# Hybrid SSD, attention and MoE block: the last two units' rows added by one-hot matrices on PE, the other rows read during these units

## What is computed

```python
    _, eidx = lax.top_k(jnp.where(emask, biased, -jnp.inf), TOP_K)        # TOP_K = 6
    w = w / jnp.sum(w, axis=-1, keepdims=True) * ROUTE_SCALE
    out = (jax.nn.silu(n @ s_gate) * (n @ s_up)) @ s_down                 # shared expert
    for e in range(N_EXPERTS):                                            # 64
        hid = jax.nn.silu(n @ e_gate[e]) * (n @ e_up[e])
        out = out + (hid @ e_down[e]) * combine[:, e:e + 1]
    ...
        h = h + g2 * ff.reshape(bsz, t, d)
    return rms_norm(h, final_g)
```

## Time and profile before

| | |
|---|---|
| median of 3 runs | 1293.59 us (1291.52 to 1294.53) |
| the profiled execution's own time | 1292.14 us |
| its span, first to last instruction | 1290.4 us |
| busy: PE, DVE, ACT, POOL | 92%, 37%, 19%, 15% |
| HBM read, written | 314.49 MB, 26.82 MB |

### The profile page before, as it was taken

How to read it: one execution, slowest core, us unless ns; L and a number is a source line. 1 busy time by engine, 2 the same in 40 slices (tenths; PEclk the granted TensorE clock), 3 DMA queues, 4 the chain that set the end, 5 groups by cost and what they waited for, 6 DMA issues and landing times. The chain is left out here.

```text
span 1290.4 us, 13395 instructions
## 1 busy us (share of the span) xinstructions
PE 1187.4 (92%) x4803; PEld 611.3 (47%) x4803; DVE 480.3 (37%) x994; ACT 246.4 (19%) x611; POOL 196.2 (15%) x320
## 2 busy tenths in 40 slices
PE   4999999998999999999999999999989999967866
PEld 2535864555554444458854444444434444423322
DVE  4686035655566211104764222233222322212225
ACT  2141122233441000001121111112111211111101
POOL 5000021111002000010351212221212121211100
PEclk9999999999999999999999999999999999988988
DMA  9742242213449232337256999999999999999647
GB/s 300 192 131 65 66 137 93 90 42 131 131 131 307 84 130 66 96 104 315 93 204 265 346 421 421 423 423 421 413 409 410 395 400 403 377 388 421 268 189 289
DMA packets 108105, 322.28 MB, mean 250 GB/s; under 512 B 14500, under 2 KB 67832, under 8 KB 81032
## 3 DMA queue, kind: packets, MB, share of 16 engines
q1 hardware_dynamic: 87824, 269.37, 54.6%
q0 software_dynamic: 18688, 47.30, 10.4%
q10 hardware_dynamic: 1528, 4.77, 1.0%
HBM read 314.49 MB, written 26.82 MB: 264 GB/s over the span
## 5 line engine op out<-in xcount | busy, mean ns | idle before, releaser
L1795 PE MATMUL ps<-gu_hi,xsT 128*64 128x512 f32 (+1 forms) x704 | 241.8, 614 | 30.1 <-DMA gu_hi<-in_exp_w_up_dram 11.6
L1795 PE MATMUL ps<-gu_lo,xsT 128*64 128x512 f32 (+1 forms) x320 | 145.8, 609 | 9.8 <-issue 6.0
L1795 PEld LDWEIGHTS ps<-gu_hi,xsT 128*64 128x64 f32 (+1 forms) x704 | 84.6, 155 | 140.2 <-issue 138.6
L1335 DVE SCALAR_TENSOR_TENSOR hid<-ps,wgt,gated 128x256 f32<-128x256 f32 x42 | 20.3, 484 | 306.9 <-ACT gated L913 306.9
L1803 PE MATMUL ps<-dn_hi,hidT 128*64 128x512 f32 (+1 forms) x352 | 119.9, 597 | 1.3 <-DVE hn L1331 1.1
L1442 PE MATMUL ps<-n1T,ring 128*128 128x512 f32 x256 | 111.9, 593 | 0.0
L1672 PE MATMUL ps<-n1T,ring 128*128 128x512 f32 x256 | 110.9, 592 | 0.7 <-ACT attT L857 0.7
L688 POOL DMA_INDIRECT expert_rows<-hn,meta x42 | 41.9, 998 | 412.8 <-DVE hn L1331 371.0
L1331 DVE TENSOR_TENSOR hn<-ps,g_row 128x1024 f32<-128x1024 f32 x42 | 51.4, 1225 | 95.2 <-PE ps L1803 95.2
L913 ACT ACTIVATE gated<-ps 128x256 f32<-128x256 f32 x42 | 16.1, 384 | 333.2 <-PE ps L1795 333.2
L1795 PEld LDWEIGHTS ps<-gu_lo,xsT 128*64 128x64 f32 (+1 forms) x320 | 51.1, 165 | 60.3 <-issue 59.8
(11 more groups left out here) (331 smaller groups left out, 1341.6 us busy)
## 6 DMA issues: line engine op xcount, KB each, us to landing
gu_hi<-in_exp_w_gate_dram SPq DMA_DIRECT2D x44, 1024.0 KB
gu_hi<-in_exp_w_up_dram SPq DMA_DIRECT2D x44, 1024.0 KB
dn_hi<-in_exp_w_down_dram SPq DMA_DIRECT2D x44, 1024.0 KB, 29.2
ring<-in_w_in_dram SPq DMA_DIRECT2D x21, 1024.0 KB, 5.5
gu_lo<-in_exp_w_gate_dram SPq DMA_DIRECT2D x20, 1024.0 KB
gu_lo<-in_exp_w_up_dram SPq DMA_DIRECT2D x20, 1024.0 KB
dn_lo<-in_exp_w_down_dram SPq DMA_DIRECT2D x20, 1024.0 KB
h<-in_ada_w_dram POOLq DMA_DIRECT2D x32, 512.0 KB, 4.8
```

Source lines behind the costliest of these rows:

```text
L1795: ins = pe.matmul(ps[rows, 2 + b, :], xsT[:, b, k, rows], gu(s)[:, :, k, :], start=(k == 0), stop=(k == KC - 1))
```

## The change

What it does, engine by engine:

- U4 and U5 are not scattered. In a round, POOL scatters the earlier round's U4 at step 0, and nothing at step 5; after the loop nothing is left to scatter.
- Since rows of these units are no longer written, ACT fills all of `expert_rows` with zeros after attention, with six 2 MB DMAs from the tile `state`, which POOL sets to zero. SP and POOL wait for them after the merge.
- SP waits for the scatters up to U3 only, then reads tiles 0 and 1 (slots 0 and 4), then final_g, then tiles 2 and 3 (slots 2 and 5). Each tile's reads wait for the units that used their slots.
- POOL writes a row of numbers 0 to 511. DVE compares it with the token number of each row of U4 and U5, which gives a 128x512 one-hot matrix for each, and adds rows 0 and 1 of tile 0 to `h`, all of it ahead of the copy of U5's rows.
- PE multiplies these matrices with `ys`, so U4's and U5's rows go to their tokens in PSUM, and adds rows 4 and 5 (tile 3: row 5) with the identity. DVE adds the other rows to `h` one by one.

```diff
--- before.py
+++ after.py
@@ -288,7 +288,10 @@
         sh_hidT = scratch[:, T * FF:T * FF + 4 * P].rearrange("p (b j c) -> p b j c", b=2, j=2)
         taken = scratch[:, 2 * FF:4 * FF].rearrange("p (t q) -> p t q", t=T)
         blank = hn[:, T - 1, :]
-        junk = gu(FIXED).rearrange("p a k f -> p (a k f)")
+        spread, junk = (gu(SLOT[SEQ0 + LAST + T + i]).rearrange("p a k f -> p (a k f)") for i in range(2))
+        spread = spread[:, 0:2 * SEQ].rearrange("p (b t) -> p b t", b=2)
+        numbers = marks[:, 0:SEQ]
+        ON_PE = ((4, 5), (4, 5), (4, 5), (5,))
         fin_g = xsT[:, 0, :, :].rearrange("p k c -> p (k c)")
 
         widths = [KC * NE, NE, TOPK * NE, NE, RGROUPS * 8, RGROUPS * RGROUPS, RGROUPS * RGROUPS, P, RGROUPS * RGROUPS,
@@ -365,6 +368,7 @@
         gu_ready, gate_done, hid_done = sem("gu_ready"), sem("gate_done"), sem("hid_done")
         ht_ready, hT_done, ey_ready, ey_dve = sem("ht_ready"), sem("hidT_done"), sem("ey_ready"), sem("ey_dve")
         tail_sum, fsq_in, fin_done, stored = sem("tail_sum"), sem("fsq_in"), sem("fin_done"), sem("stored")
+        zeroed, numbered, spread_done = sem("zeroed"), sem("numbered"), sem("spread_done")
         block = ctx.enter_context(nc.Block())
 
         def block_used(n):
@@ -385,7 +389,8 @@
 
         def two_rows(t, part):
 
-            return flat(dn(t)) if part == 2 else gu(t)[:, part, :, :].rearrange("p k f -> p (k f)")
+            s = SLOT[SEQ0 + LAST + t]
+            return flat(dn(s)) if part == 2 else gu(s)[:, part, :, :].rearrange("p k f -> p (k f)")
 
         def rows_in_part(t, part):
 
@@ -448,6 +453,7 @@
                 load_block(n)
 
             sp.wait_ge(merged_done, KC)
+            sp.wait_ge(zeroed, 16 * TOPK)
             sp.dma_start(r_w[:, :, :], a["router_w"][0].rearrange("(p k) e -> p k e", k=KC)).then_inc(small_in, 16)
             sp.dma_start(r_b, a["router_bias"][0:1, :].broadcast_to([P, NE])).then_inc(small_in, 16)
             sp.dma_start(sh_gu[:, 0, :, :], a["sh_w_gate"][0].rearrange("(p k) f -> p k f", k=KC)).then_inc(shared_in, 16)
@@ -509,17 +515,26 @@
                     for i in range(2):
                         load_dn(slots[i], ids[i])
             units, each = count * LAST + BEFORE, count * (16 * LAST // 2) + 16 * BEFORE // 2
-            sp.to_reg(units), sp.to_reg(each)
+            others, free = each - 16, [units - 2, units - 1]
+            sp.to_reg(units), sp.to_reg(others), sp.to_reg(free[0]), sp.to_reg(free[1])
+            rows_v = rows_d.rearrange("(t p k) d -> p t (k d)", p=P, k=TOPK)
+
+            def read_rows(t):
+                sp.wait_ge(gu_ready, free[t // 2])
+                for part in range(3):
+                    if part == 2:
+                        sp.wait_ge(ey_ready, free[t // 2])
+                    sp.dma_start(two_rows(t, part), rows_v[:, t, 2 * D * part:2 * D * part + 2 * D]).then_inc(rows_in_part(t, part)[0], 16)
+
+            for b in range(2):
+                sp.wait_ge(scattered[b], others)
+            for t in range(2):
+                read_rows(t)
             sp.wait_ge(exT_act, units + 1)
             sp.wait_ge(exT_dve, units + 1)
             sp.dma_start(fin_g, a["final_g"].rearrange("(o d) -> o d", o=1).broadcast_to([P, D])).then_inc(fin_in, 16)
-            for b in range(2):
-                sp.wait_ge(scattered[b], each)
-            sp.wait_ge(ey_ready, units)
-            rows_v = rows_d.rearrange("(t p k) d -> p t (k d)", p=P, k=TOPK)
-            for t in range(T):
-                for part in range(3):
-                    sp.dma_start(two_rows(t, part), rows_v[:, t, 2 * D * part:2 * D * part + 2 * D]).then_inc(rows_in_part(t, part)[0], 16)
+            for t in range(2, T):
+                read_rows(t)
             for t in range(T):
                 sp.wait_ge(fin_done, t + 1)
                 sp.dma_start(out_v[:, t, :], h[:, t, :]).then_inc(stored, 16)
@@ -598,6 +613,7 @@
                 pool.tensor_tensor(urs[:, :], urs[:, :], mhalf[:, 0:GROUPS], ALU.pow).then_inc(root_done, 1)
 
             pool.wait_ge(uT_ready, T)
+            pool.memset(state[:, :], 0.0).then_inc(const, 1)
             for n in range(NLATE):
                 if n >= 4:
                     pool.wait_ge(late_used, n - 3)
@@ -605,6 +621,7 @@
                     .then_inc(late_in[n % 4], 16)
 
             pool.wait_ge(merged_done, KC)
+            pool.wait_ge(zeroed, 16 * TOPK)
             pool.memset(blank, 0.0).then_inc(rconst_step, 1)
             pool.memset(low[:, :, :], 1.0).then_inc(rconst_step, 1)
             pool.memset(pay[:, :, :, :], 0.0).then_inc(rconst_step, 1)
@@ -713,8 +730,10 @@
                     pool.wait_ge(sy_ready, T)
                     pool.dma_start(lo[:, 2:, :], list_v[:, 2:, :]).then_inc(lists_rest, 16)
                     pool.dma_start(hi[:, 2:, :], list_v[:, 2:, :]).then_inc(lists_rest, 16)
-                if un >= 1:
+                if 1 <= un < BEFORE - 1:
                     scatter((un - 1) % 6, (un - 1) % 2, un)
+            pool.iota(numbers, [[1, SEQ]], base=0, channel_multiplier=0,
+                      allow_small_or_imprecise_dtypes=True).then_inc(numbered, 1)
             count = load_turns(pool)
             with pool.Fori(0, count) as j:
                 for m in range(LAST):
@@ -723,12 +742,16 @@
                     col = from_table(j, m + 2)
                     pool.to_reg(done), pool.to_reg(ready), pool.to_reg(copied), pool.to_reg(filled), pool.to_reg(col)
                     pool.wait_ge(lists_rest, 32)
+                    if m == 0:
+                        in_front = done - 1
+                        pool.to_reg(in_front)
+                        scatter(LAST - 2, 0, in_front)
                     pool.wait_ge(exT_ready, ready)
                     gather((m + 2) % 6, m % 2, col, copied, filled)
-                    scatter((m - 1) % 6, (m - 1) % 2, done)
+                    if m < LAST - 1:
+                        scatter((m - 1) % 6, (m - 1) % 2, done)
             units, each = count * LAST + BEFORE, count * (16 * LAST // 2) + (16 * BEFORE // 2 + 16)
             pool.to_reg(units), pool.to_reg(each)
-            scatter(5, 1, units)
             for b in range(2):
                 pool.wait_ge(gathered[b], each)
             for t in range(T):
@@ -856,6 +879,10 @@
                 act.wait_ge(att_ready, c + 1)
                 act.activation(attT[:, :, CHUNK * c:CHUNK * c + CHUNK],
                                ps[:, 0, :].rearrange("p (j q) -> p j q", q=CHUNK), ACT.Copy).then_inc(att_done, 1)
+            act.wait_ge(const, 4 + 2 * PAIRS)
+            to_zero = rows_d.rearrange("(q p n) d -> q p n d", p=P, q=TOPK)
+            for q in range(TOPK):
+                act.dma_start(to_zero[q], state[:, :].unsqueeze(1).broadcast_to([P, SEQ // P, D])).then_inc(zeroed, 16)
             for i in range(D // WB):
                 for b in range(2):
                     for jj in range(2):
@@ -1397,6 +1424,26 @@
                     rows_out((m - 1) % 2, at)
                     upper((m + 3) % 6, from_table(j, m + 3))
             units = count * LAST + BEFORE
+            def spread_rows(b):
+
+                token = sums[:, 12 + b:13 + b]
+                chain(dve.tensor_copy(token, meta[:, LAST - 2 + b, 0:1]))
+                dve.tensor_scalar(spread[:, b, :], numbers, token, None, ALU.is_equal).then_inc(spread_done, 1)
+
+            def add_row(t, k):
+                if k % 2 == 0:
+                    dve.wait_ge(*rows_in_part(t, k // 2))
+                chain(dve.tensor_tensor(h[:, t, :], h[:, t, :], two_rows(t, k // 2)[:, D * (k % 2):D * (k % 2) + D], ALU.add))
+
+            dve.wait_ge(numbered, 1)
+            copied = units * 2
+            dve.to_reg(copied)
+            dve.wait_ge(meta_done, copied)
+            dve.wait_ge(gu_ready, units)
+            for b in range(2):
+                spread_rows(b)
+            for k in range(2):
+                add_row(0, k)
             dve.wait_ge(scattered[1], count * (16 * LAST // 2) + 16 * (BEFORE // 2 - 1))
             rows_out(1, units)
 
@@ -1407,10 +1454,9 @@
                                          op0=ALU.mult, op1=ALU.mult).then_inc(fin_done, 1)
 
             for t in range(T):
-                total = dn(t)[:, 0, :]
-                dve.wait_ge(*rows_in_part(t, 2))
-                chain(dve.tensor_tensor(total, total, dn(t)[:, 1, :], ALU.add))
-                chain(dve.tensor_tensor(h[:, t, :], h[:, t, :], total, ALU.add))
+                for k in range(2 if t == 0 else 0, TOPK):
+                    if k not in ON_PE[t]:
+                        add_row(t, k)
                 dve.wait_ge(tail_sum, t + 1)
                 dve.tensor_tensor(h[:, t, :], h[:, t, :], flat(ps[:, 2 * t:2 * t + 2, :]), ALU.add).then_inc(fsq_in, 1)
                 if t >= 1:
@@ -1897,18 +1943,33 @@
                 pe.wait_ge(dn_in[SLOT[r]], count * (16 * 2 * LAST // SLOTS) + 16 * (NTH[r] - 2 * LAST // SLOTS))
```

(29 more changed lines are left out.)

## The result

The changed kernel takes 1286.01 us (median of 4 runs, 1284.22 to 1287.94), against 1293.61 us for the kernel before, measured beside it: ratio 0.9943, 95% interval 0.9928 to 0.9957. It is faster by 7.6 us. The forecast was 1286.5 with a range of 1284.0 to 1291.0.

The account below looks back on a forecast made before the run. DVE's row adds were taken to bound the tail: 1248.3+2.51+2x7.73+6.25+10.78 = 1283.3 against 1290.4, 7.1 less, with early reads and zeroing at nothing. This gave 1285.0 for the profiled execution, 1286.5 as median, range 1284 to 1291.

Parts of the forecast that it names:

- The sum: Tail after U5's down: PE's tile 0 sum at 1248.3, then DVE's work to 1283.3, against 1290.4, so 7.1 less.
- The early reads: SP, near U5's start: first read issued at 1222.5, landed at 1227.5, all parts near 1255; no cost to U5.
- price the rival: Early reads come late, DVE's first add holding up U5's copy: 1.6 to 9.6 us lost; chance 0.09.
- later by X-1239.3: DVE before U5's copy: if the first read part lands at X after 1239.3, the end is later by that difference.
- what the rival would have cost: PE's clock falls in the tail: ten matmuls at the lower level make tile 0 8.7 later, median about 1295; chance 0.07.
- The zeroing: Six 2 MB DMAs on ACT's queue after attention, 2.8 us to issue, transfers meeting POOL's late loads; taken as costing nothing.
- The bound for the transfers: POOL's late loads beside the zeroing: with even sharing, 20 us become about 40 at worst, last load at 439.
- the prediction's worst case: Three queues at a third each during zeroing: 60 us from 400 give 460, a loss of 21 and 1307.
- zeroing stalls PE: Rival at PE's wait for the late sums at 441: late loads delayed by zeroing make PE wait; chance 0.20.
- Its threshold of 438.5: Late loads before PE's wait at 441: each microsecond the last one lands after 438.5 is one lost.
- Its own list of the changed profile: Expected signs: reads near 1222, no clock below 1.0 after 1225, DVE waiting only for tile 0's square, PE done 7 us ahead.
- PE and not DVE ends the tail: Rival in the tail: DVE's adds overlap better, the end is 1276.5 and the median 1279.7; chance 0.04.

Follow-up runs that it names:

- the row move: Against the changed kernel, PE instead of DVE adds rows 3 and 4 of tile 3 too; 1281.81 us, ratio 0.9914 to the kernel before.
- the run with late reads: Against the changed kernel, SP waits for U5's last down matmul before its first read of expert_rows; 1293.28 us, ratio 0.9996 to the kernel before.
- The two runs with late reads: Changed kernel with SP's reads held until U5's last down matmul: 1293.28 us; the same with the copy of U5's rows ahead of all row adds: 1292.51 us.
- the doubled run: Against the changed kernel, twelve zeroing DMAs instead of six, the second six to an unread spare tensor; 1313.47 us, ratio 1.0156 to the kernel before.
- The adds ahead: Against the changed kernel, DVE adds rows of tiles 0 and 1 before waiting for PE's tile 0 sum, staying two tiles ahead; 1279.4 us, ratio 0.9888.

## Why the prediction was right, and where its steps were off

**The tail.** The sum gave 44.0 from the end of U5's down part, and it was 43.4. Its terms: PE begins with no gap where 0.34 was put, and tile 0's sum is there 8.9 after its start (1242.72 to 1251.58), as computed (1239.6 to 1248.3 is 8.7). The PSUM adds are 7.54, 7.53 and 8.79 apart; the sum had 2.51+5.0, 7.73 and 2.73+6.25 = 8.98. From the last to the end 10.66 pass, against 10.78. That DVE and not PE ends the tail is shown by the row move (2.4 for two adds), and PE is 6.8 ahead, where "some 7" was written.

**The early reads.** The step was right, one of its numbers was not. The scatter of U3 was taken to land 2.6 after its issue, since the DMA share was low. It is issued at 1223.30 and SP's first read follows at 1229.59, with that scatter named as what SP waited for, so it took up to 6.3. With the 4.9 that a first part needs in the run with late reads (1242.17 to 1247.06), the rows are there at about 1234.5, an estimate. The prediction let DVE's first add begin as late as 1239.3 at no cost, just at the end of U5's down part, which is 1242.8 in this profile. So the margin is about 8 us and not 12. It was enough, and the add, at 1240.38, names no DMA. The experiments price the rival: late reads cost 7.2, where the rule "later by X-1239.3" gives 5.0. In the scale of that rule, the first add began 5.0 after the end of U5's down part (1242.06). The rule has the length of PE's wait about right (5.4), and lacks what the lower clock adds behind it (1.6).

**The clock.** No window of the tail is below 1.00; only 1225 to 1230 has 0.74, which is U5's beginning after its wait for weights, as in the earlier trace rows. The two runs with late reads show what the rival would have cost: after 5.4 idle, two matmuls took 1.6 more, after 4.85 four took 2.95 more. TensorE: Matmul & The Clock Gate of the Trainium skill (HAM oscillation) has waits for data bring the slow level back; both traces agree, and the changed kernel without such a wait keeps the full clock.

**The zeroing.** That it would cost nothing held, and one term of it was mis-sized by far: "ACT's own 2 MB DMA takes 0.47 to issue; six are 2.8". They took 32.6. The price of one DMA that was issued alone was multiplied by six, though it is near the truth only for the first three (0.62 to 1.53 each) and the others took 10.62, 11.06 and 7.07. It cost nothing only because of the cover that the prediction named beside it, that PE needs that gate 35 us later. That the term came out at nothing is the cover's doing and not its working's. Measured, the cover left is some 9 us, and the doubled run shows the loss behind it (28). The bound for the transfers was fairer: the last late load was put at 439 at worst and its sum began at 432.68. The sums name a wait for their load each time and come 2.95 apart (426.79, 429.66, 432.68), so POOL's queue moved 0.5 MB per 2.95 us beside ACT's full queue. The rows of the queues say the same: 1.77 of 4.16 MB in 10 us, near 43%. DMA: Bandwidth & Descriptors of the Trainium skill (Queues, rings and completion order) has each DMA engine go round its queues packet by packet; the trace agrees, with 481, 481 and 480 packets for the three queues. The sharing is even in packets and not in bytes: SP's are about 1 KB (0.49 MB in 480), the others near 4 KB. This is why POOL had more than the third which the prediction's worst case gave it. The rival "zeroing stalls PE" had its place a little wrong. The wait that comes first, in the doubled run, is the one for ACT's gate at 444.4, right behind the matmuls on the late sums. Its threshold of 438.5 is also 1.3 too early: DVE's 1.28 ahead of 441.07 leave 439.8. Nothing came near it.

**What the forecast did not say** is that 6.3 us more lay in the order of DVE's adds. Its own list of the changed profile had DVE waiting for PE's sum of tile 0 at 1248.3 with 13 adds still to do. The price was there too, under the rival "PE and not DVE ends the tail": 1279.7 as a median. The adds ahead, in which DVE comes only 0.4 behind PE, measured 1279.4.

## What to carry to other kernels

When a way through memory is hidden, work out which engine is next, and give that engine in its remaining wait whatever work is already ready: here adds whose rows had landed stood behind a wait for a sum, and moving them was worth almost as much as the change itself. A DMA's issue time taken alone is no price for several large ones in a row on a compute engine's queue; here only three went out at once, and every further one cost the time in which the queue moves one transfer. Look for who needs that engine. Before moving work between two engines, see how far the other one is ahead: the same edit gave 2.4 us and cost 3.0, depending on 6.8 or 0.4 of lead.

## What was not expected of the hardware

- Issuing large DMAs can hold the issuing engine for about as long as they take to move. Of the 2 MB transfers in a row on ACT's queue, the first three took 0.6 to 1.7 us each to issue; the following ones took 7 to 12 while POOL's loads shared the DMA engines or had just ended, and 4.7 to 6.2 later. In sum: 0.5 us for one, 1.3 to 2.7 for two, 12.2 for four, 32.6 for six and 67 for twelve.
- Three queues that all had work moved equal numbers of packets (481, 481, 480 in 10 us), and so bytes in the ratio of their packet sizes.
- A wait of PE of some 5 us in the midst of dense work was enough for the lower clock: the next two matmuls took 1.6 us more after 5.4 idle, the next four 2.95 more after 4.85. After the 25 us of the doubled run it was not more (2.6).
